# Last stage of a hybrid decoder step: rows transposed as they are, the norm's factor put on per token at the copy out of PSUM

## The reference

```python
def rmsnorm(x, g):
    xf = x.astype(jnp.float32)
    y = xf * lax.rsqrt(jnp.mean(xf * xf, axis=-1, keepdims=True) + NORM_EPS)
    return (y * g.astype(jnp.float32)).astype(x.dtype)
...
    y_prompt = rmsnorm(hp, norm_f)
    y_sample = rmsnorm(hs, norm_f)
```

## Time and profile before

| | us |
|---|---|
| median of 3 runs (2658.54 to 2666.04) | 2665.42 |
| the profiled execution | 2663.28 |
| its span, from first to last record | 2661.5 |
| TensorE, matrix products | 2322.6 (87% of the span) |
| TensorE, weight loads | 1675.2 (63%) |
| VectorE | 729.0 (27%) |
| ScalarE | 328.0 (12%) |
| GpSimd | 73.2 (3%) |

### The profile page before, as it was taken

How to read it: one execution, slowest core, us unless ns; L and a number is a source line. 1 busy time by engine, 2 the same in 40 slices (tenths; PEclk the granted TensorE clock), 3 DMA queues, 4 the chain that set the end, 5 groups by cost and what they waited for, 6 DMA issues and landing times. The chain is left out here.

```text
span 2661.5 us, 48885 instructions
## 1 busy us (share of the span) xinstructions
PE 2322.6 (87%) x21073; PEld 1675.2 (63%) x21073; DVE 729.0 (27%) x2022; ACT 328.0 (12%) x744; POOL 73.2 (3%) x124
## 2 busy tenths in 40 slices
PE   5899999799999867786776986999999989999996
PEld 4576677677777666765544765556665656655663
DVE  1111111400141144445654124221121111222115
ACT  1001100201210000013321001101010100010101
POOL 0000000000000000001011001000000000000000
PEclk9999999899999967676978996999999999999998
DMA  9887885613344420026568106999999999999990
GB/s 324 341 320 271 335 336 198 179 64 127 116 130 132 118 81 5 5 58 151 190 253 339 66 0 256 426 425 422 419 427 420 425 424 422 423 426 419 421 405 37
DMA packets 205117, 687.64 MB, mean 258 GB/s; under 512 B 38986, under 2 KB 85019, under 8 KB 165371
## 3 DMA queue, kind: packets, MB, share of 16 engines
q1 hardware_dynamic: 195746, 642.59, 61.9%
q0 software_dynamic: 7056, 38.29, 4.3%
q10 hardware_dynamic: 2180, 4.76, 0.5%
HBM read 687.16 MB, written 19.86 MB: 266 GB/s over the span
## 5 line engine op out<-in xcount | busy, mean ns | idle before, releaser
L2711 PE MATMUL bank<-sb_gate_w,sb_x_picked 128*64 128x256 f32 x2048 | 331.7, 390 | 53.2 <-DMA sb_up_w<-in_w_up_dram 53.2
L690 PE MATMUL bank<-sb_hT,sb_sample_kv 128*128 128x296 f32 (+1 forms) x1408 | 355.4, 412 | 12.3 <-PEq L494 12.3
L2711 PE MATMUL bank<-sb_up_w,sb_x_picked 128*64 128x256 f32 x2048 | 329.8, 388 | 0.0
L690 PEld LDWEIGHTS bank<-sb_hT,sb_sample_kv 128*128 128x128 f32 x1408 | 268.1, 191 | 94.6 <-issue 17.7
L2711 PEld LDWEIGHTS bank<-sb_gate_w,sb_x_picked 128*64 128x64 f32 x2048 | 174.7, 141 | 126.3 <-issue 83.1
L2736 PE MATMUL bank<-sb_down_w,sb_hiddenT 128*64 128x512 f32 x1024 | 226.8, 595 | 9.0 <-ACT sb_x_picked L2793 9.0
L469 PE MATMUL bank<-sb_cmp_xT,sb_cmp_w 128*128 128x254 f32 x1024 | 223.3, 379 | 6.6 <-ACT sb_cmp_xT L241 5.8
L469 PEld LDWEIGHTS bank<-sb_cmp_xT,sb_cmp_w 128*128 128x128 f32 x1024 | 193.3, 190 | 38.1 <-ACT sb_cmp_xT L241 8.3
L2711 PEld LDWEIGHTS bank<-sb_up_w,sb_x_picked 128*64 128x64 f32 x2048 | 178.4, 141 | 50.6 <-issue 3.8
L2863 DVE TENSOR_TENSOR sb_hidden<-sb_hidden,bank 128x256 f32<-128x256 f32 x32 | 13.5, 421 | 685.8 <-ACT sb_hidden L2801 685.8
L2736 PEld LDWEIGHTS bank<-sb_down_w,sb_hiddenT 128*64 128x64 f32 x1024 | 84.2, 137 | 128.9 <-issue 115.3
(11 more groups left out here) (563 smaller groups left out, 2367.7 us busy)
## 6 DMA issues: line engine op xcount, KB each, us to landing
sb_gate_w<-in_w_gate_dram SPq DMA_DIRECT2D x64, 2048.0 KB, 16.6
sb_up_w<-in_w_up_dram SPq DMA_DIRECT2D x64, 2048.0 KB, 21.1
sb_down_w<-in_w_down_dram SPq DMA_DIRECT2D x64, 2048.0 KB
sb_w_ada<-in_w_ada_dram SPq DMA_DIRECT2D x48, 2048.0 KB, 10.9
sb_sample_kv<-in_w_in_dram SPq DMA_DIRECT2D x22, 2048.0 KB, 8.1
sb_sample_kv<-in_cache_cmp_kv_dram SPq DMA_DIRECT2D x128, 256.0 KB, 7.4
sb_sample_kv<-in_w_out_dram SPq DMA_DIRECT2D x16, 1024.0 KB, 10.9
sb_sample_kv<-in_state_win_kv_dram SPq DMA_DIRECT2D x8, 1024.0 KB, 17.1
```

The source lines that it names most:

```text
L690: ins = pe.matmul(bank[j % 4][:, 0:wide], ch[:, t, j % 2 * P:(j % 2 + 1) * P], hT[:, t, 0:wide], start=(t == 0), stop=(t == KT - 1))
L2711: ins = pe.matmul(bank[b][64 * half:64 * half + 64, col:col + 256], x[:, t, b * 64:b * 64 + 64], w[i][:, t % CK, half * 256:half * 256 + 256],
```

## The change

The last stage is written anew; all phases before it stay.

- The samples' gated add becomes two operations over all sixteen tiles, ahead of the prompt's sixteen adds.
- ScalarE squares the tiles in place of VectorE. A copy of each tile times the gain is written to `k.acc`: for the tiles with `m % 8 < 5` (ten) by ScalarE, for the other six by VectorE. The factor is left out of it.
- TensorE takes the products of four tiles and then transposes the blocks of these four tiles for the three row groups, and so on by quarters; blocks 0 to 6 of the twelve are transposed so, into seven banks (`HELD`), before the factor is known. A block is now numbered quarter first, row group second.
- The root is padded to 384 columns by GpSimd and turned by three products with one column of the identity, so that the factor stands as one number per partition for each row group; VectorE inverts these 128 x 3 numbers out of bank 0.
- The copies out of PSUM multiply by that factor. Blocks 7 to 11 are transposed when banks come free.
- SP writes each row group in two halves of 1024 features, six transfers in all.
- ScalarE takes a root of one column at the start of the stage.

```diff
--- before.py
+++ after.py
@@ -2882,71 +2882,104 @@
 
 def phase_final(k, A):
 
+
     nc = k.nc
+    HELD = 7
     with ExitStack() as c:
         sb = lambda name, shape, dt=F32: k.sb(name, shape, dt, c)
-        sq, part = sb("f_squares", [P, KT, NT]), sb("f_gated", [P, 2, NS])
-        rstd, sd = sb("f_rstd", [P, NT]), sb("f_root", [P, NT])
-        rows = k.h2rows
-        s_q, s_s, s_sd = k.s_norm
-        before = k.norms
-        s_n = k.sem("f_normed")
-        s_t, s_o = k.sem("f_transposed"), k.sem("f_out")
+        sq, part, sd, rstd = sb("f_squares", [P, KT, NT]), sb("f_gated", [P, KT, NS]), sb("f_root", [P, NTT * P]), sb("f_rstd", [P, NTT])
+        rows, spare = k.h2rows, sb("f_spare", [P, 1])
+        s_a, s_q, s_g, s_s, s_sd, s_k, s_v = (k.sem("f_" + n) for n in ("added", "squared", "scaled", "summed", "rooted", "turned_root", "dve"))
+        s_f, s_t, s_o = k.sem("f_factor"), k.sem("f_transposed"), k.sem("f_out")
+        s_gd, s_pad = k.sem("f_scaled_dve"), k.sem("f_root_padded")
         s_r = [k.sem("f_rows_act"), k.sem("f_rows_dve")]
+        on_act = lambda m: m % 8 < 5
         with nc.Block() as block:
-            def copies(eng, copy, parity):
+            def turned_copies(eng, copy, parity):
                 for n in range(parity, 4 * NTT, 2):
-                    i, q = divmod(n, 4)
+                    q, i = divmod(n, NTT)
                     r = ROWS[i][1]
                     eng.wait_ge(s_t, n + 1)
-                    copy(rows[0:r, i, q * 512:(q + 1) * 512], k.bank[1 + n % 4][0:r, :]).then_inc(s_r[parity], 1)
+                    copy(rows[0:r, i, q * 512:(q + 1) * 512], k.bank[1 + n % HELD][0:r, :], rstd[0:r, i:i + 1]).then_inc(s_r[parity], 1)
 
             @block.vector
             def _(dve):
-                step = k.steps.chain(dve)
+                step = Chain(dve, s_v)
+                by_t = lambda v: v.rearrange("p k (b t) -> p k b t", t=TS)
+                gate = k.mod[:, 80:80 + KT, 1:NC].unsqueeze(3).to_broadcast([P, KT, NB, TS])
+                step(dve.tensor_tensor(by_t(part[:, :, :]), by_t(k.acc[:, :, TP:NT]), gate, ALU.mult))
+                step(dve.tensor_tensor(k.xT[:, :, TP:NT], k.xT[:, :, TP:NT], part[:, :, :], ALU.add))
                 for m in range(KT):
-                    step(add_gated(k, dve, step, m, k.acc[:, m, 0:TP], k.acc[:, m, TP:NT], 80, part[:, m % 2, :]))
-                    dve.tensor_tensor(sq[:, m, :], k.xT[:, m, :], k.xT[:, m, :], ALU.mult).then_inc(s_q, 1)
-                dve.wait_ge(s_sd, before + 1)
-                step(dve.reciprocal(rstd[:, :], sd[:, :]))
-                for m in range(KT):
-                    dve.scalar_tensor_tensor(out=k.acc[:, m, :], in0=k.xT[:, m, :], scalar=k.par[:, C_NORMF + m:C_NORMF + m + 1],
-                                             in1=rstd[:, :], op0=ALU.mult, op1=ALU.mult).then_inc(s_n, 1)
-                copies(dve, dve.tensor_copy, 1)
+                    dve.scalar_tensor_tensor(out=k.xT[:, m, 0:TP], in0=k.acc[:, m, 0:TP], scalar=k.mod[:, 80 + m, 0:1],
+                                             in1=k.xT[:, m, 0:TP], op0=ALU.mult, op1=ALU.add).then_inc(s_a, 1)
+                    if not on_act(m):
+                        dve.wait_ge(s_a, m + 1)
+                        dve.tensor_scalar(k.acc[:, m, :], k.xT[:, m, :], k.par[:, C_NORMF + m:C_NORMF + m + 1], None, ALU.mult)\
+                           .then_inc(s_gd, 1)
+                dve.wait_ge(s_k, 1)
+                dve.reciprocal(rstd[:, :], k.bank[0][:, NT:NT + NTT]).then_inc(s_f, 1)
+                dve.wait_ge(s_f, 1)
+                turned_copies(dve, lambda out, in_, f: dve.tensor_scalar(out, in_, f, None, ALU.mult), 1)
 
             @block.tensor
             def _(pe):
-                for t in range(KT):
-                    pe.wait_ge(s_q, before * KT + t + 1)
-                    ins = pe.matmul(k.bank[0][:, 0:NT], k.ones[:, :], sq[:, t, :], start=(t == 0), stop=(t == KT - 1))
-                ins.then_inc(s_s, 1)
-                for n in range(4 * NTT):
-                    i, q = divmod(n, 4)
+                for q in range(4):
+                    for t in range(4 * q, 4 * q + 4):
+                        pe.wait_ge(s_q, t + 1)
+                        ins = pe.matmul(k.bank[0][:, 0:NT], k.ones[:, :], sq[:, t, :], start=(t == 0), stop=(t == KT - 1))
+                    if q == 3:
+                        ins.then_inc(s_s, 1)
+                    for i, (at, r) in enumerate(ROWS):
+                        n = NTT * q + i
+                        if n < HELD:
+                            pe.wait_ge(s_g, sum(on_act(m) for m in range(4 * q + 4)))
+                            pe.wait_ge(s_gd, sum(not on_act(m) for m in range(4 * q + 4)))
+                            for j in range(4):
+                                ins = pe.transpose(k.bank[1 + n][0:r, j * P:(j + 1) * P], k.acc[:, 4 * q + j, at:at + r], k.ident[:, :])
+                            ins.then_inc(s_t, 1)
+                pe.wait_ge(s_sd, 1)
+                pe.wait_ge(s_pad, 1)
+
+                for i, (at, r) in enumerate(ROWS):
+                    ins = pe.matmul(k.bank[0][:, NT + i:NT + i + 1], sd[:, i * P:(i + 1) * P], k.ident[:, 0:1], start=True, stop=True)
+                ins.then_inc(s_k, 1)
+                pe.wait_ge(s_g, sum(on_act(m) for m in range(KT)))
+                pe.wait_ge(s_gd, sum(not on_act(m) for m in range(KT)))
+                for n in range(HELD, 4 * NTT):
+                    q, i = divmod(n, NTT)
                     at, r = ROWS[i]
-                    if n < 4:
-                        pe.wait_ge(s_n, 4 * (n + 1))
-                    else:
-                        pe.wait_ge(s_r[n % 2], n // 2 - 1)
+                    pe.wait_ge(s_r[(n - HELD) % 2], (n - HELD) // 2 + 1)
                     for j in range(4):
-                        ins = pe.transpose(k.bank[1 + n % 4][0:r, j * P:(j + 1) * P], k.acc[:, 4 * q + j, at:at + r],
-                                           k.ident[:, :])
+                        ins = pe.transpose(k.bank[1 + n % HELD][0:r, j * P:(j + 1) * P], k.acc[:, 4 * q + j, at:at + r], k.ident[:, :])
                     ins.then_inc(s_t, 1)
+
+            @block.gpsimd
+            def _(pool):
+                pool.memset(sd[:, NT:NTT * P], 1.0).then_inc(s_pad, 1)
 
             @block.scalar
             def _(act):
-                act.wait_ge(s_s, before + 1)
-                act.activation(sd[:, :], k.bank[0][:, 0:NT], ACT.Sqrt, bias=k.eps[:, 0:1], scale=1.0 / D)\
-                   .then_inc(s_sd, 1)
-                copies(act, act.copy, 0)
+                act.activation(spare[:, :], k.eps[:, 0:1], ACT.Sqrt)
+                for m in range(KT):
+                    act.wait_ge(s_a, m + 1)
+                    act.activation(sq[:, m, :], k.xT[:, m, :], ACT.Square).then_inc(s_q, 1)
+                    if on_act(m):
+                        act.activation(k.acc[:, m, :], k.xT[:, m, :], ACT.Copy, scale=k.par[:, C_NORMF + m:C_NORMF + m + 1]).then_inc(s_g, 1)
+                act.wait_ge(s_s, 1)
+                act.activation(sd[:, 0:NT], k.bank[0][:, 0:NT], ACT.Sqrt, bias=k.eps[:, 0:1], scale=1.0 / D).then_inc(s_sd, 1)
+                act.wait_ge(s_f, 1)
+                turned_copies(act, lambda out, in_, f: act.activation(out, in_, ACT.Copy, scale=f), 0)
 
             @block.sync
             def _(sp):
                 out = (A["y_prompt"][0, 0:P, :], A["y_prompt"][0, P:TP, :], A["y_sample"].rearrange("b t d -> (b t) d"))
-                for i, (_, r) in enumerate(ROWS):
-                    for p in range(2):
-                        sp.wait_ge(s_r[p], 2 * (i + 1))
-                    sp.dma_start(out[i], rows[0:r, i, :]).then_inc(s_o, 16)
-                sp.wait_ge(s_o, 16 * NTT)
+                for half in range(2):
+                    for i, (_, r) in enumerate(ROWS):
+                        for n in (NTT * 2 * half + i, NTT * (2 * half + 1) + i):
+                            sp.wait_ge(s_r[n % 2], n // 2 + 1)
+                        cols = slice(half * D // 2, (half + 1) * D // 2)
+                        sp.dma_start(out[i][:, cols], rows[0:r, i, cols]).then_inc(s_o, 16)
+                sp.wait_ge(s_o, 16 * 2 * NTT)
                 sp.wait_ge(k.s_kept, 16)
```

## The result

| | before | after |
|---|---|---|
| median, beside each other on one chip | 2665.5 us (2658.54 to 2666.04) | 2648.72 us (2644.27 to 2653.28) |
| ratio, 95% interval | | 0.9947, 0.9927 to 0.9967 |
| the same, repeated with more runs (`e9_after_again`) | 2664.42 us (2651.05 to 2671.26) | 2649.68 us (2642.53 to 2658.5) |
| ratio of the repetition | | 0.9945, 0.9929 to 0.996 |
| profiled execution: time, span | 2663.28, 2661.5 us | 2644.27, 2642.5 us |

The changed kernel is faster by 0.53% by the ratio, some 14 us; the first pair of medians lies 16.8 us apart, the repeated pair 14.7. 2651 us was forecast, within 2645 to 2658, and "faster by over 0.3%".

What follows compares the result with a forecast made beforehand. TensorE was taken as the last stage's new bound. Sum 3.5 us sooner, reciprocal 1.8 and scalings 7.0 less, turning 0.9 more, copies the rest, transfers 0.8 back: 13.4 us less, 2651 us put down, range 2645 to 2658.

Steps and rivals of the forecast that it cites:

- VectorE's adds: Start of last stage: two whole operations 1.4 us, then sixteen adds 0.44 apart, 0.92 for six tiles with scaled copies, 9.9 us.
- ScalarE's squares: Last stage: squares at 0.39 us, copies with gain at 0.42; ten tiles of both 8.1 us, six squares alone 2.3.
- (c): Rival: ScalarE reloads its function table between square and scaled copy, twenty loads, 25.7 us; 9.8 us more, 2675; chance 0.03.
- (d): Rival: square and root don't share a ScalarE table, two loads, 2.6 us; 2654.5 on the median; chance 0.10.
- TensorE as the new bound: Products and 28 transposes in TensorE's in-order queue set the sum of squares, at 2637.7, 3.5 us sooner than before.
- Rival (a): TensorE stays at 1.2 GHz through the whole last stage: only 3.1 us less, 2662 on the median; chance 0.06.
- the bound of 2.8 for a clock up from the start: TensorE's products and transposes up to the sum: 2.8 us less if the clock is up from the start.
- Rival (e): The edit doesn't bring the sum forward, transposes standing before it: 9.9 us left, 2655.5; chance 0.04.
- The factor: After the sum: root 0.51 us, three turning products 0.9, reciprocal 0.16 for 1.96; sixteen scalings, 6.97 us, leave the path.
- The copies: Out of seven full banks: 0.69 us each on VectorE, 0.585 and 0.10 on ScalarE; last ends at 2643.6, against 2657.77.
- The output: Six transfers from 2640.7, 1.4 us plus 5.6 for 2.36 MB and 0.35 to the span's end, 2648.1.
- rival (b): The six output transfers run one behind the other: 16.6 us from 2640.7, 2661.6 on the median; chance 0.05.

Runs made afterwards that it cites:

- e9_after_again: The changed kernel run once more with nothing edited: last stage 27.8 us, ratio 0.9945 to the kernel before.
- e6_new_adds: Kernel before plus only the samples' adds in two operations and squares on ScalarE, everything from the root on as before: last stage 33.3 us against 40.6.
- e3_products_first: Changed kernel with all sixteen products of the sum first, then the 28 transposes, then the turning products: last stage 26.8 us against 27.9.
- e4_held4: Changed kernel with four blocks transposed ahead of the factor instead of seven: last stage 27.7 us against 27.9.
- e5_old_adds: Changed kernel with VectorE adding and squaring tile by tile as before, ScalarE only writing copies with the gain: last stage 32.1 us against 27.9.
- e7_early_products: Changed kernel with six products of constants on TensorE before the first square is there: last stage 26.1 us against 27.9.
- e10_spread_rows: Changed kernel with the two 32-row transfers reading every fourth of 128 partitions instead of 32 neighbours: last stage 26.9 us against 27.9.
- e2_no_sample_rows: Changed kernel without the two transfers of the 32 sample rows: last stage 26.0 us against 27.9.
- e8_all_four: Changed kernel with early constant products, products first, four held blocks, four later constant products, samples' rows in one transfer: stage 25.35 us against 27.9, ratio 0.9951 to before.

## Why the prediction was right

The forecast, counted from the stage's start, against the trace:

| step | forecast | after | before |
|---|---|---|---|
| VectorE's two operations over all tiles done | 1.4 | 1.4 | |
| first product starts | 2.3 | 2.5 | 1.4 |
| clock at 2.4 GHz | 7.9 | 7.8 | 7.0 |
| VectorE through with adds and scalings | 11.3 | 10.3 | |
| ScalarE's last square | 12.3 | 11.7 | |
| sum of squares | 16.8 | 16.2 | 20.4 |
| factor per token (before: its reciprocal) | 18.4 | 17.85 | 22.9 |
| first transfer issued | 19.8 | 19.4 | 31.9 |
| last copy done | 22.7 | 21.9 | 36.9 |
| end | 27.2 | 27.9 | 40.6 |

*VectorE's adds* were right in kind, a little too long: six take 2.46 us, the last of them 0.48, so they stand 0.395 apart for the 0.44 taken, and the scaled copy costs its whole place: some 0.80 us from one such tile to the next (2618.81, 2619.62, 2620.41 on VectorE's timeline), so another 0.4. Nothing of it shows, since TensorE is later.

*ScalarE's squares*: 0.33 us apart for the 0.39 taken from the root of the same shape. ScalarE was done 4.5 us ahead of the sum, as forecast. Rivals (c) and (d), a table load between square and copy or ahead of the root, fall with the one load at 2614.54. The Trainium skill (ScalarE: Activation LUTs, Table sets) does not list the square with the root; the trace shows them with no load between.

*TensorE as the new bound* held: its chain has no gap for squares, and the clock rose 5.4 us after the first product, for 5.6. The size came out 0.6 us too long, mostly by the transposes: twelve took 1.31 us at 2.4 GHz, 0.11 each, where I took 0.13 from a row only mostly at that clock. Products took 0.49 for 0.50 there, and 1.05 for 1.0 at 1.2 GHz. `e6_new_adds` and `e3_products_first` confirm the step that the sum stands behind the 28 transposes: 3.3 us. Rival (a), 1.2 GHz throughout, fell with the rise at 2622.4; the low clock up to there costs 2.9 us by after's own rows, and the bound of 2.8 for a clock up from the start was near that. Rival (e) fell: the sum came 4.2 us sooner.

*The factor*: 1.63 us from sum to factor for 1.6.

*The copies*: a scaled copy takes the place of 0.67 us on VectorE (six in 4.03) and 0.59 on ScalarE (3.53), for 0.69 and 0.685. They did not wait for a block, where the sum had the last copy behind the last block, 0.2 us late by its own terms. The clock did not fall in them, as it did in `e4_held4`, `e5_old_adds` and `e7_early_products`; the 2.9 us that the prediction held ready for this case as a bound were not needed, and 1.1 to 1.5 is what it cost where it came for 20 transposes.

*The output* is the mis-sized term: 7.4 us from first issue to end were forecast and 8.6 measured; from last copy to end 6.0 for 4.5. The transfers did overlap, against rival (b), and the form of the sum was right, one start and then a stream of bytes. But I put all bytes at the 418 GB/s of a transfer out of 128 partitions. `e10_spread_rows` gives 0.9 of the 1.2 us to the two transfers out of 32 neighbours; for the rest there is the steady rate of some 400 GB/s, 5.9 us for 2.36 MB instead of 5.6.

So the sum's two errors, 0.8 us too long up to the last copy and 1.5 too short behind it, leave 12.7 for 13.4. The mechanism was right; that the two errors have opposite signs, and so the total comes out closer than its parts, is luck. Where the 12.7 us came from, by the same table: 4.2 us up to the sum, 0.9 between sum and factor, 10.0 from there to the last copy (scalings off the path, seven full banks), and 2.3 back in the output, which now waits for the stream and not for the last copy.

Three things stay open: what makes the clock fall in the copies of some runs and not of others; why it rose 4.6 us after the first product in `e2_no_sample_rows` and 5.6 in before and `e5_old_adds`, which moves the stage by some tenths; and whether more than scatter stands behind the 6.3 us ahead of the stage. A layout that holds the samples' own rows in partitions further apart was not tried.

## What to carry to other kernels

A factor per row or column that is only known after a long reduction can be put on at the last copy, and everything up to that copy then runs before the factor is there; what was on the path is left as a few small operations. Work moved ahead in an in-order queue must be counted into what stands behind it (3.3 us here), and best put where the engine would wait anyway, as beside the root. Where a stage's gain is less than the scatter of what lies ahead of it, read its length in the trace, not the total alone.

## What the runs showed of the hardware

- Two 128 KB transfers out of 32 neighbouring partitions lowered the rate of all queues together, to 270 GB/s for a microsecond from 406, and lengthened the 512 KB beside them from 3.6 to 4.0 us. The same bytes out of every fourth partition left it at 393 to 418 in the microseconds after the copies.
- SP's own issue of a 128 KB transfer took 0.73 us right behind two others in after and 1.4 right behind five; in before it was 0.34 for 256 KB, 1.4 us behind the last and with that one still under way.
- The granted clock fell to 1.2 GHz within the copies in `e4_held4`, `e5_old_adds` and `e7_early_products`, though TensorE was at work again; it stayed at 2.4 GHz through the copies in after and its repetition, `e3_products_first` and `e8_all_four`.
- A square of 128x288 stands 0.33 us before the next operation on ScalarE, a copy with a gain per partition 0.42; a root of that shape took 0.39.
